# Transposing a norm's result inside the product before it, and half of a layer norm's affine step on GpSimd

## The reference

```python
# first block, its end
x = x + merged @ w_out
h2 = rms_norm(x, g_mlp)
x = x + jnp.square(jax.nn.relu(h2 @ w_up)) @ w_down
# twice
mixed = jnp.concatenate([fox_out, ret_out], axis=-1)
x = layernorm(DEEPNORM_ALPHA * x + mixed @ w_out, ln1_g, ln1_b)
hid = jnp.square(jax.nn.relu(x @ w_ff1))
x = layernorm(DEEPNORM_ALPHA * x + hid @ w_ff2, ln2_g, ln2_b)
```

## Time and profile before

| | |
|---|---|
| median of 3 runs | 1271.27 us (1271.05 to 1272.31) |
| the profiled execution | 1271.03 us |
| its span, first to last instruction | 1269.2 us |
| busy | PE 1225.7 us (97%), PEld 1085.8 (86%), DVE 769.7 (61%), ACT 608.6 (48%), POOL 0.2 |
| DMA | 217 MB, 171 GB/s over the span |
| granted PE clock, mean | 0.997 of full speed |

### The profile page before, as it was taken

How to read it: one execution, slowest core, us unless ns; L and a number is a source line. 1 busy time by engine, 2 the same in 40 slices (tenths; PEclk the granted TensorE clock), 3 DMA queues, 4 the chain that set the end, 5 groups by cost and what they waited for, 6 DMA issues and landing times.

```text
span 1269.2 us, 18459 instructions
## 1 busy us (share of the span) xinstructions
PE 1225.7 (97%) x7568; PEld 1085.8 (86%) x7568; DVE 769.7 (61%) x853; ACT 608.6 (48%) x679; POOL 0.2 (0%) x4
## 2 busy tenths in 40 slices
PE   5999999999999999999989999999999999999997
PEld 4979998988888789899788878999988977899895
DVE  5566875674565665545366686555565677755555
ACT  4565554665444454444355445543435544544441
POOL 0000000000000000000000000000000000000000
PEclk9999999999999999999999999999999999999999
DMA  5644354444565355555253454645516345365550
GB/s 204 237 167 167 114 176 143 170 140 154 215 215 184 133 199 199 197 192 173 95 206 133 141 199 169 230 166 197 186 66 243 138 141 199 133 232 180 188 194 33
DMA packets 33533, 217.31 MB, mean 171 GB/s; under 512 B 4416, under 2 KB 6464, under 8 KB 7744
## 3 DMA queue, kind: packets, MB, share of 16 engines
q1 hardware_dynamic: 33472, 216.44, 48.1%
HBM read 215.37 MB, written 1.05 MB: 171 GB/s over the span
## 4 chain that ended last, share of the span: by engine, by line
PE 73%; DVE 12%; DMA 7%; ACT 5%; issue 2%; SPq 0%; ACTq 0%; DVEq 0%
PE gps L1291 27%; DMA raw<-w 7%; PE aps L1330 7%; PE aps L1331 7%; PE aps L1336 7%; PE gps L1330 6%; PE gps L1331 6%; PE gps L1336 6%; DVE w_lo L730 5%; ACT w_hi L335 3%; DVE B L878 1%; PE aps L1449 1%; DVE rs L868 1%; DVE B L872 1%; DVE B L822 1%
## 5 line engine op out<-in xcount | busy, mean ns | idle before, releaser
L730 DVE TENSOR_TENSOR w_lo<-raw,w_hi 128x2048 fp32r<-128x2048 f32 x200 | 449.1, 2249 | 292.7 <-ACT w_hi L335 291.6
L335 ACT ACTIVATE w_hi<-raw 128x2048 fp32r<-128x2048 f32 x200 | 374.9, 1877 | 233.2 <-DMA raw<-w 121.6
L1291 PE MATMUL gps<-R_hi,w_hi 128*128 128x256 f32 x736 | 192.5, 283 | 0.0
L1291 PE MATMUL gps<-R_hi,w_lo 128*128 128x256 f32 x736 | 192.3, 283 | 0.0
L1291 PE MATMUL gps<-H_hi,w_hi 128*128 128x256 f32 x640 | 172.7, 291 | 11.5 <-ACT H_hi L370 5.9
L1291 PE MATMUL gps<-H_hi,w_lo 128*128 128x256 f32 x640 | 169.3, 286 | 0.0
L1330 PE MATMUL aps<-w_hi,Q_hi 128*128 128x512 f32 x416 | 162.6, 391 | 2.4 <-DVE Q_lo L928 1.8
L1331 PE MATMUL aps<-w_lo,Q_hi 128*128 128x512 f32 x416 | 162.2, 390 | 0.0
L1291 PE MATMUL gps<-R_lo,w_hi 128*128 128x256 f32 x736 | 147.6, 283 | 0.0
L1291 PEld LDWEIGHTS gps<-R_hi,w_lo 128*128 128x128 f32 x736 | 141.2, 192 | 0.8
L1291 PEld LDWEIGHTS gps<-R_hi,w_hi 128*128 128x128 f32 x736 | 141.1, 192 | 0.8
(11 more groups left out here) (212 smaller groups left out, 1426.9 us busy)
## 6 DMA issues: line engine op xcount, KB each, us to landing
raw<-w SPq DMA_DIRECT2D x196, 1024.0 KB, 4.8
B<-rows SPq DMA_DIRECT2D x4, 1024.0 KB, 4.7
B<-x_t SPq DMA_DIRECT2D x2, 512.0 KB, 4.6
B<-mem_t SPq DMA_DIRECT2D x1, 1024.0 KB, 7.6
B<-x SPq DMA_DIRECT2D x1, 1024.0 KB, 7.5
B<-con SPq DMA_DIRECT2D x1, 1024.0 KB, 9.0
out<-B SPq DMA_DIRECT2D x4, 256.0 KB, 2.0
B<-rows SPq DMA_DIRECT2D x1, 512.0 KB, 6.9
```

Source lines behind the costliest of these rows:

```text
L335: act.activation(w_hi[:, ring(l), 0:n], raw[:, raw_slot(l), 0:n], ACT.Copy)\
L730: dve.tensor_tensor(w_lo[:, ring(l), 0:n], raw[:, raw_slot(l), 0:n], w_hi[:, ring(l), 0:n].bitcast(F32), ALU.subtract)\
L1291: return pe.matmul(gps[:, bank_, nt * T:(nt + 1) * T], w[:, r, c:c + P], op[:, k, :], start=start, stop=stop, skip_group_check=True)
```

## The change

Three things are edited. First, `turn` transposes one chunk i = 2m + j instead of both chunks of a tile, and is called from inside `tokens_part`, between its eight high matmuls and its four low ones (`between`): chunk 0 in the last product before the norm, chunks 1, 2 and 3 in the first three of the four products after it. ACT and DVE go along with it chunk by chunk. Second, in a layer norm chunk 1 of each tile is no longer finished by DVE but by POOL, with three instructions, released by a new semaphore `t_root` when the root is there. `t_z` becomes two semaphores, one for each chunk. Third, a few splits trade places: in the MLP, half `l0 + 5` is split after the first `up_hi` and `up_lo`; before LN0 and LN2 the halves `LFFN` and `LFFN + 1` are split between the steps of `gn_hi` and `gn_lo`.

```diff
@@ scalar @@
             def mlp_norm():
-                for m in range(2):
-                    for j in range(2):
-                        act.wait_ge(s["resid"], 2 * m + j + 1)
-                        act.activation(dump[:, j, :], chunk(X, m, j), ACT.Square, scale=1.0 / 32,
-                                       accum_out=stats[:, m, 20 + j:21 + j]).then_inc(s["t_sq"], 1)
-                    root_start(0, m)
-                    turn_hi(N_MLP, m, R_hi)
+                def squared(m, j):
+                    act.wait_ge(s["resid"], 2 * m + j + 1)
+                    act.activation(dump[:, j, :], chunk(X, m, j), ACT.Square, scale=1.0 / 32,
+                                   accum_out=stats[:, m, 20 + j:21 + j]).then_inc(s["t_sq"], 1)
...
+                squared(0, 0)
+                squared(0, 1)
+                root_start(0, 0)
+                turn_hi(N_MLP, 0, R_hi)
+                squared(1, 0)
+                turn_hi(N_MLP, 1, R_hi)
+                squared(1, 1)
+                root_start(0, 1)
+                turn_hi(N_MLP, 2, R_hi)
+                turn_hi(N_MLP, 3, R_hi)
...
                 split(h0, l0 + 4)
-                split(h0, l0 + 5)
                 up_hi(n, ub, 0)
                 up_hi(n, ub, 1)
+                split(h0, l0 + 5)
@@ vector, mlp_norm @@
                 added(1, 0)
                 turn_lo(N_MLP, 0, R_hi, R_lo)
                 added(1, 1)
+                turn_lo(N_MLP, 1, R_hi, R_lo)
                 rooted(1)
-                turn_lo(N_MLP, 1, R_hi, R_lo)
+                turn_lo(N_MLP, 2, R_hi, R_lo)
+                turn_lo(N_MLP, 3, R_hi, R_lo)
@@ vector, layer_norm @@
                     root(1 + n, m)
+                    dve.sem_inc(s["t_root"], 1)
                     finished(m, 0)
-                    centred(m, 1)
-                    st.settle()
-                    finished(m, 1)
+                    if m and hi is not None:
+                        turn_lo(i, 1, hi, lo)
...
@@ vector, END @@
+            ended(0, 0)
+            ended(0, 1)
+            ended(1, 0)
+            turn_lo(N_END, 0, H_hi, H_lo)
+            ended(1, 1)
+            for i in range(1, 4):
+                turn_lo(N_END, i, H_hi, H_lo)
...
@@ new, gpsimd @@
+            for n in range(2 * LAYERS):
+                g_row, b_row = ln_rows[n % 2][:, 0, 512:1024], ln_rows[n % 2][:, 1, 512:1024]
+                pool.wait_ge(s["rows_loaded"], 16 * (n + 2))
+                for m in range(2):
+                    t = chunk(X, m, 1)
+                    pool.wait_ge(s["t_root"], 2 * n + m + 1)
+                    st.mark(pool.tensor_scalar(t, t, stats[:, m, 12:13], stats[:, m, 17:18], ALU.subtract, ALU.mult))
+                    st.settle()
+                    st.mark(pool.tensor_tensor(t, t, g_row, ALU.mult))
+                    st.settle()
+                    pool.tensor_tensor(t, t, b_row, ALU.add).then_inc(s["t_z1"], 1)
@@ tensor, tokens_part @@
                     pe.matmul(out, x, w_lo[:, r, c], start=False, stop=False)
+                if between is not None:
+                    turn(*between)
                 if lo_ready is not None:
                     pe.wait_ge(*lo_ready)
@@ tensor, tokens_after_norm @@
                 for m in range(2):
-                    turn(n, m, src, ready, count)
                     for g in range(2):
+                        i = 2 * m + g
                         pe.wait_ge(s["lo_ready"], h0 + (l + g + 1))
...
-                                          stop=(g == 1), hi_ready=(s["nhi"], c), lo_ready=(s["nlo"], c))
+                                          stop=(g == 1), hi_ready=(s["nhi"], c), lo_ready=(s["nlo"], c),
+                                          between=(n, i + 1, src, ready, count) if i < 3 else None)
```

More of the change, by code:

```diff
@@ L619, in _ @@
             ffn(0, FFN1, 0)
-            for m in range(2):
-                turn_hi(N_END, m, H_hi)
+            for i in range(4):
+                turn_hi(N_END, i, H_hi)
             split_gates(HALVES1, 0)
@@ L713, in _ @@
                                .then_inc(s["gn_hi"], 1)
-                        split(h0, LFFN)
-                        split(h0, LFFN + 1)
+                            split(h0, LFFN + m)
                 layer_norm(ly * 2, R_hi)
@@ L806, in root, with turn_lo @@
                 newton(v, r0, a, r, None)
[L808 to L814, removed]
+            def turn_lo(n, i, hi, lo):
+                m, j = i // 2, i % 2
+                dve.wait_ge(s["nhi"], 4 * (n + 2) + i + 1)
+                dve.tensor_tensor(operand(lo, m, j), four(turned(m, j)),
+                                  operand(hi, m, j).bitcast(F32), ALU.subtract)\
+                   .then_inc(s["nlo"], 1)
             def residual(m, j, out, scale):
@@ L904, in layer_norm @@
                 if hi is not None:
-                    turn_lo(i, 1, hi, lo)
+                    turn_lo(i, 2, hi, lo)
+                    turn_lo(i, 3, hi, lo)
             def up(uu, par_, a):
@@ L1125, in _, with ended @@
             ffn(0, FFN1, 0)
[L1126 to L1130, removed]
+            def ended(m, j):
+                sum_done(N_END, m, j, HALVES1)
+                residual(m, j, acc(m, j), None)
+            ended(0, 0)
[5 more added lines that the diff above has]
+                turn_lo(N_END, i, H_hi, H_lo)
             for a in range(2):
@@ L1269, in _ @@
                 gn_lo(0)
+                split(h0, LFFN)
                 gn_lo(1)
-                split(h0, LFFN)
                 split(h0, LFFN + 1)
@@ L1347, in tokens_half, with turn @@
                     .then_inc(s["gemm_done"], 1)
-            def turn(n, m, src, ready, count):
-                for j in range(2):
-                    pe.wait_ge(ready, count + 2 * m + j + 1)
-                    for k in range(4):
-                        ins = pe.transpose(turned(m, j)[:, k * P:(k + 1) * P],
-                                           chunk(src, m, j)[:, k * P:(k + 1) * P], ident)
-                    ins.then_inc(s["t_tr"], 1)
+            def turn(n, i, src, ready, count):
+                m, j = i // 2, i % 2
+                if ready is s["resid"]:
+                    pe.wait_ge(ready, count + i + 1)
+                else:
+                    pe.wait_ge(ready[j], count // 2 + m + 1)
+                for k in range(4):
+                    ins = pe.transpose(turned(m, j)[:, k * P:(k + 1) * P],
+                                       chunk(src, m, j)[:, k * P:(k + 1) * P], ident)
+                ins.then_inc(s["t_tr"], 1)
             def turn_merged(j, m):
@@ L1383, in sum_tiles, with ffn @@
                 return ins
-            def ffn(h0, l0, n, src, ready, count):
+            def ffn(h0, l0, n, src, ready, count, after):
                 ub = 16 * n
@@ L1409, in last_down @@
                             pe.wait_ge(s["lo_ready"], h0 + (l + a + 1))
-                            ins = tokens_part(l + a, acc(m, a), m, par_, Q_hi, Q_lo, stop=True)
+                            ins = tokens_part(l + a, acc(m, a), m, par_, Q_hi, Q_lo, stop=True,
+                                              between=after if m and a else None)
                             ins.then_inc(s["acc_ready" if m == 0 else "gemm_done"], 1)
```

47 lines of the change are left out of this document (28 added, 19 removed).

## The result

| | before | after |
|---|---|---|
| median | 1271.16 us (1270.76 to 1272.31, 4 runs) | 1284.95 us (1284.27 to 1286.05, 4 runs) |
| the profiled execution | 1271.03 us | 1285.57 us |
| PE busy | 1225.7 us | 1230.9 us |
| DVE, POOL busy | 769.7, 0.2 us | 761.7, 42.1 us |

The change makes the kernel 1.07% slower: the ratio is 1.0107, with a 95% interval of 1.0092 to 1.0122. The forecast was 1272.8, with a range up to 1277.8.

What follows compares the result with a forecast made beforehand. PE was taken to bound the kernel. Terms 1.14 + 1.15 + 0.89 + 0 - 0.79 - 1.28 + 0.42 gave 1.5 us over the profiled 1271.03, so 1272.6, median 1272.8; range 1268.8 to 1277.8.

Steps and rivals of the forecast that it cites:

- What POOL costs: Layer norms: three POOL instructions at 1.1 us each, 3.7 from root to finished (2.6 to 7.3); hidden except at LN3, 0.4 later.
- the sum: All places' terms added: 1.5 us more than the profiled 1271.03, so 1272.6, and 1272.8 for the median.
- Rival 2: POOL late above 4.0 us, PE standing at T1 and T3: 1276.6 us at 4.6, 1297 at 7.3; chance 0.25.
- The rhythm: Groups of transposes T0 to T3, one per chunk, come 3.18 us apart, T3 9.54 after T0; no wait for copies.
- The weights: PE waits 1.4 us for `w_lo` before `rows_first` at three places, and over 4 us behind END and LN1.
- the terms of MLP and END: `rows_first` at MLP starts 1.14 us later; PE's wait for weights behind END ends 1.15 us later.
- the second kind of wait: PE's waits past the transposes: 2.22 us for `w_lo` behind END, 0.63 and 1.12 for `Q_lo` behind LN0 and LN2.
- The moved split: In the MLPs behind LN0 and LN2, PE no longer waits for half `l0 + 5`: 0.79 and 1.28 us less.
- LN3: At the kernel's end the second residual starts 1.04 us earlier, but with POOL's work LN3 ends 0.4 us later.
- Rival 3: PE's clock falls behind the longer waits at END and LN1, 0.5 us counted for each: 1273.8 us; chance 0.10.
- Rival 1: The waits at the transposes, some 8 us, are the gain: 1264 us, or 1268.5 with half of it; chance 0.10.

Runs made afterwards that it cites:

- e1: The changed kernel with the affine step of chunk 1 back on DVE and POOL doing nothing: 1277.0 us, ratio 1.0038 to the kernel before.
- e4: The changed kernel with the two small halves (gates) split behind the first copy at END and LN1, not the fourth: 1277.87 us.
- e6: The kernel before with only splits moved (gates at END and LN1, half `l0 + 5` in the MLP): 1264.22 us, ratio 0.9936.
- e9: e6 with `LFFN` split between the two `gn_lo` and `LFFN + 1` behind DVE's first residual; transposes outside the products: 1261.12 us, ratio 0.991.
- e2: The changed kernel, but POOL begins a chunk only when DVE has finished chunk 0 of the same tile: 1287.63 us.
- e11: The kernel before with only POOL's affine step of chunk 1 added, in place of DVE's: 1294.75 us, ratio 1.0174.
- e7: The changed kernel with DVE's affine step (e1), gates early (e4), `l0 + 2` and `LFFN + 1` splits moved: 1260.21 us, ratio 0.9904 to before.
- e5: e1 with chunk 0 at LN0 and LN2 transposed behind the last product's four low matmuls again: 1275.04 us, ratio 1.0019 to before.
- e8: As e2, but POOL's first instruction takes a different form at each of eight places; run for durations alone, no kernel time given.
- e10: e7 with the affine step of chunk 1 on POOL again: 1278.16 us, ratio 1.0048 to the kernel before.
- e3: The changed kernel with POOL's first instruction taking two constants in place of the mean and the root: 1281.61 us.

## Why the prediction was wrong, step by step

- **What POOL costs** is the step that failed. I priced the three instructions alike, at 1.1 us by DVE's rows for like sizes, and took 3.7 us from root to finished. The two `tensor_tensor` took 1.26 to 1.30 alone, near enough; the first took 2.08 and waited 0.55 besides. From the root it is 5.5 us to a finished chunk. The upper bound of 7.3 held it; I chose by size where the form decided. The wait of 0.55 for `finished` was named in the prediction, at up to 0.75, and then put at nothing in the sum, since no row could show it. Without POOL (e1) 8.0 us of the 13.8 are gone, so this step is shown to be the cause of that much.
- **Rival 2** was the right mechanism, PE behind POOL at T1 and T3 with the second root behind ACT's copy of chunk 1. With its own rule and 5.5 us it gives 1.5 + 1.4 at LN0 and LN2, 1.1 + 1.4 at LN1 and 1.8 at LN3 over the forecast, 10.1 in all, where the traces show 11.4. With the DVE step that POOL held up at LN3 (1.07) it is 11.2. That it comes out so well at LN0 is partly luck: there T1 is as late by the clock as by POOL. At the upper bound of 7.3 us the same rule gives 22.7 over, 1295.5, and not the 1297 of the prediction. The rival should have had more than 0.25, and the range, which left out its far half, should have reached to it.
- **The rhythm**: T0 to T3 is 9.87 us at END (620.75 to 630.62) against 9.54, since the first matmul behind a group of transposes takes 0.31 and not 0.23. MLP has the wait of 0.60 for chunk 2 (0.9 forecast). No wait for a copy is left.
- **The weights**: 1.04 and 1.07 us for `w_lo` before `rows_first` at MLP and LN0 (1.4 forecast), 4.15 and 4.22 behind END and LN1 (over 4): right, and the terms of MLP and END with them. "Whether time is won depends on the second kind of wait" is what e4, e6 and e9 show: moving splits alone gives 0.6 to 0.9%.
- **The moved split** of `l0 + 5`: -0.83 and -1.29 against -0.79 and -1.28. No wait for `Q_lo` is left.
- **LN3**: the second residual came 1.01 earlier in the row (1.04 forecast), and the root lost it again to POOL.
- **Rival 3**, the clock: behind LN1 it cost 0.50, as counted, behind END nothing. At LN0 it fell for 1.7 us of work, which was not forecast and runs beside POOL's work in the changed kernel; in e1 it is bare.
- **Not of the change**, as far as the traces tell: 1.84 us at the start. PE waits there for ACT behind a load, at 82 us: 1.86 us in before and 2.38 after, with the clock at 0.83 behind it. In the traces of e2 and e4, whose code there is the same, it stays up, and they reach the place of 416.89 at 414.95 and 414.66. The kernel before has the fall too: e9 and e11 have its code up to MLP, and their traces show a granted clock of 0.83 over the 10 us from 80 and reach MLP's first transposes 1.7 us later than the trace of before. In all, 9 of the 13 traces have it and 4 have not, with the same code there. So most of this 1.84 is a difference between two traces and not the change. The -0.19 before LN2 is 0.50 of clock and -0.69 behind it (1058.96 to 1075.29 before, 1069.27 to 1084.91 after): the wait at T0 was 1.61 us in the trace of before and 1.08 in e6, with the same code.
- **Rival 1** had no time to win: e7 and e9 differ by 0.8 us.

Open is when the clock falls. With it goes most of e1's distance from the sum, 5.9 us above before where 1.1 was forecast: its trace is over the forecast by 1.6 us at the start and 1.8 at LN0, the two places of the lower clock, by 0.9 at LN2 and 0.4 at LN1 (the rhythm, and the wait for DVE at LN2), and by less elsewhere. The change itself makes the wait in front of T0 at LN0 longer, from 1.07 to 1.99 us, since the low matmuls no longer stand before it; whether that makes the fall more likely was not settled by e5 and e6.

## What to carry to other kernels

Price an instruction that the trace doesn't show by its form on that engine, not by its size on another, and where the bounds are 2.6 and 7.3 us around a slack of 4.0, forecast the side that holds more of them. Before work is moved to GpSimd, look at what VectorE does in the same microseconds: each instruction of VectorE with two operands in SBUF can hold up GpSimd or be held up by it, whichever the path needs. A wait at a transpose is worth taking away only when the weights and the small loads behind it come earlier too; here moving a few splits gave the gain, with or without the new transposes.

## What the runs showed of the hardware

- GpSimd on 128x512 float32: `tensor_tensor` 1.26 to 1.30 us, with one value a partition broadcast 1.04; `tensor_scalar` with two operations 1.94 (constants) and 2.08 (one value a partition), with one 1.50 and 1.57; copy 0.61 (e2, e8).
- VectorE and GpSimd hold each other up when GpSimd reads SBUF and VectorE's instruction has two operands there: 0.55 us for GpSimd at `finished` (e2), 2.05 for GpSimd behind the split of 2.29 (e10), 1.07 for a step on 128x1 (LN3). `turn_lo` and the residuals, which read one operand from PSUM, keep their 0.69 beside GpSimd.
- Behind a `tensor_tensor` of GpSimd this is a wait for its end: `centred`, 0.74 us alone, ends 1.81 to 1.85 us after the start of GpSimd's 1.26 to 1.30 us whenever it starts within them, in all 17 cases in the traces (1.47 us long in the lines of LN2 above, 1.80 in e2 where it starts 0.02 us behind). Behind GpSimd's `tensor_scalar` with constants it is not: `finished` is 0.38 us longer and ends 0.77 before it (e3).
- The Trainium skill (SBUF — State Buffer, Who interferes with whom) has the exclusion as its rule, an exclusive lock in which the order of issue decides who is blocked. The traces agree for `tensor_tensor`, e3 fits only in part, and the prediction gave the rule's sum without taking it. The figure that the prediction takes from the Trainium skill, about twice VectorE's time (GPSIMD Engine Reference, Performance versus the Vector engine), is that of an addition: the estimate of 1.1 us for 512 elements stands beside 1.28 measured for such an instruction, and the first of the three is of another form.
- The granted clock falls to half for a few microseconds behind waits of about 2 us, but the same code and like waits (LN0 and LN2 in before and in e6) had it in one trace and not in the other: a mean of 0.83 over 10 us in e6 (waits of 1.07 and 0.80 us), and 1.00 in before (1.07 and 0.79 at LN0, 1.61 and 0.80 at LN2).
